# A hybrid-attention decoder layer on one core: VectorE takes the maxima of a new unit before it divides a finished one

## The reference

```
h = x @ w_in + b_in
qa, ka, va, qb, kb, vb, qc, z = split(h)
oa = banded attention(rope(qa), rope(ka), va, window 128, sinks)   # branch a, 8 heads, 2 key heads
ob = dilated attention(rope(qb), rope(kb), vb,                     # branch b, 4 heads
                       (window, stride) = (128,1), (512,4), (2048,16))
oc = attention(qc, mem @ wk, mem @ wv)                             # branch c, 4 heads, 256 keys
y  = concat(rms(oa), rms(ob), rms(oc)) * g * silu(z)
out = layer_norm(alpha * x + y @ w_out)
# within attention: s = q k / 8;  m = max(s);  p = exp(s - m);  o = (p / sum(p)) v
```

## Time and profile before

| | |
|---|---|
| median of 3 runs (lowest, highest) | 500.43 us (500.07, 501.27) |
| the profiled execution's own time | 500.67 us |
| its span, first to last instruction | 498.5 us |
| TensorE matmul busy | 488.8 us, 98% |
| VectorE busy | 311.0 us, 62% |
| ScalarE busy | 226.6 us, 45% |
| mean granted TensorE clock | 0.996 |

### The profile page before, as it was taken

How to read it: one execution, slowest core, us unless ns; L and a number is a source line. 1 busy time by engine, 2 the same in 40 slices (tenths; PEclk the granted TensorE clock), 3 DMA queues, 4 the chain that set the end, 5 groups by cost and what they waited for, 6 DMA issues and landing times.

```text
span 498.5 us, 9771 instructions
## 1 busy us (share of the span) xinstructions
PE 488.8 (98%) x3526; PEld 448.3 (90%) x3526; DVE 311.0 (62%) x893; ACT 226.6 (45%) x511; POOL 70.8 (14%) x52
## 2 busy tenths in 40 slices
PE   8999999999999999999999999999999999999994
PEld 7999999999999988888888888899888898888883
DVE  4878644557565853434534468876767868877734
ACT  5632222112211134564545659947374656454540
POOL 0000000000000000111101100023232323231414
PEclk9999999999999999999999999999999999999998
DMA  7984453547632344532331258723333424232022
GB/s 283 376 255 127 159 180 104 193 134 248 212 126 87 105 125 131 158 99 75 95 97 50 98 164 266 233 58 104 114 101 106 135 68 151 67 116 83 1 85 84
DMA packets 51838, 67.97 MB, mean 136 GB/s; under 512 B 9552, under 2 KB 41296, under 8 KB 51792
## 3 DMA queue, kind: packets, MB, share of 16 engines
q1 hardware_dynamic: 51216, 66.31, 41.6%
q10 hardware_dynamic: 576, 1.05, 0.6%
HBM read 51.31 MB, written 16.02 MB: 135 GB/s over the span
## 4 chain that ended last, share of the span: by engine, by line
PE 90%; DVE 3%; ACT 3%; DMA 1%; issue 1%; SPq 0%; DVEq 0%; ACTq 0%
PE long_ps L1032 16%; PE o_ps L979 10%; PE wide L846 8%; PE wide L845 8%; PE wide L844 8%; PE narrow L961 5%; PE long_ps L921 5%; PE long_ps L923 5%; PE long_ps L922 5%; PE wide L949 4%; PE wide L950 3%; PE wide L855 2%; PE wide L857 2%; PE wide L856 2%; DMA x_raw<-in_x_t 1%; PE narrow L1008 1%
## 5 line engine op out<-in xcount | busy, mean ns | idle before, releaser
L846 PE MATMUL wide<-x_hi,w_lo 128*128 128x256 f32 x320 | 89.6, 280 | 0.0
L844 PE MATMUL wide<-x_hi,w_hi 128*128 128x256 f32 x320 | 89.3, 279 | 0.0
L845 PE MATMUL wide<-x_lo,w_hi 128*128 128x256 f32 x320 | 89.3, 279 | 0.0
L845 PEld LDWEIGHTS wide<-x_lo,w_hi 128*128 128x128 f32 x320 | 60.2, 188 | 0.0
L846 PEld LDWEIGHTS wide<-x_hi,w_lo 128*128 128x128 f32 x320 | 60.1, 188 | 0.0
L1113 ACT ACTIVATE spill<-turn 128x512 fp32r<-128x512 f32 x21 | 13.3, 632 | 102.7 <-DVE turn L1349 76.6
L844 PEld LDWEIGHTS wide<-x_hi,w_hi 128*128 128x128 f32 x320 | 59.8, 187 | 0.0
L1622 POOL TENSOR_TENSOR g_lo<-g_raw,g_hi 128x1024 fp32r<-128x1024 f32 x6 | 14.3, 2387 | 268.5 <-ACT g_hi L1118 268.5
L1032 PE MATMUL long_ps<-wo_hi,y_hi 128*128 128x512 f32 (+1 forms) x128 | 52.2, 408 | 0.0
L1032 PE MATMUL long_ps<-wo_lo,y_hi 128*128 128x512 f32 (+1 forms) x128 | 51.4, 402 | 0.0
L1032 PE MATMUL long_ps<-wo_hi,y_lo 128*128 128x512 f32 (+1 forms) x128 | 50.8, 397 | 0.0
(11 more groups left out here) (189 smaller groups left out, 1234.4 us busy)
## 6 DMA issues: line engine op xcount, KB each, us to landing
q_spill<-spill SPq DMA_DIRECT2D x32, 256.0 KB, 2.5
q_pair<-q_spill SPq DMA_DIRECT2D x128, 64.0 KB, 2.0
w_raw<-in_w_qkv SPq DMA_DIRECT2D x12, 512.0 KB, 5.0
x_raw<-in_x_t SPq DMA_DIRECT2D x16, 256.0 KB, 8.0
g_raw<-in_w_gate SPq DMA_DIRECT2D x8, 512.0 KB, 4.1
q_pair<-q_spill SPq DMA_DIRECT2D x32, 128.0 KB, 2.8
q_pair<-q_spill SPq DMA_DIRECT2D x128, 32.0 KB, 1.8
wo_raw<-in_w_out SPq DMA_DIRECT2D x8, 512.0 KB, 4.7
```

The costliest lines, as they stand in the source:

```text
L844: pe.matmul(dst, w_hi[s][:, k, f], t_hi[:, k, cols], start=(k == 0), stop=False)
L845: pe.matmul(dst, w_hi[s][:, k, f], t_lo[:, k, cols], start=False, stop=False)
L846: mm = pe.matmul(dst, w_lo[s][:, k, f], t_hi[:, k, cols], start=False, stop=(k == KT - 1))
```

## The change

In VectorE's loop the call of `unit_max` moves ahead of the calls of `unit_out`. No instruction is added or removed, and the other engines' lists stay as they are.

```
             for v in range(ITERATIONS):
+                if 0 <= v - 1 < n_units:
+                    unit_max(v - 1)
                 for u in outs_at(v):
                     unit_out(u)
-                if 0 <= v - 1 < n_units:
-                    unit_max(v - 1)
                 if 0 <= v - 2 < n_units and two_tiles(v - 2):
                     unit_sides(v - 2)
```

## The result

The change makes the kernel slower: 518.75 us median of 4 runs (518.37 to 519.33) against 500.38 (500.07 to 501.27), ratio 1.0368, 95% interval 1.0354 to 1.0382, so 18.4 us. The forecast was 516, range 509 to 521. The profiled execution after took 519.33, 0.6 over the median, with a span of 517.2 us.

What follows compares the result with a forecast made beforehand. TensorE, with matmuls in flight 98% of the span, was taken to bound the kernel. Terms 13.2 + 2.1 + 2.0 - 1.5 = 15.8 on the profiled 500.67 gave 516.5, less 0.24, 516 us; range 509 to 521.

Steps and rivals of the forecast that it cites:

- The maxima can't begin earlier: In iteration 72, maxima start 0.83 us after the iteration's first score matmul (T), only 0.06 earlier, not the quotient's 0.65.
- Who waits: At each iteration's end times_v on TensorE waits for the quotient, as o_ps exists once; about 28 times, 15 to 20 us.
- Far units, 13.2: 16 branch-b units with merges, blocks 4 to 7: quotient behind maxima and merges delays the values' matmuls, 13.2 us together.
- ready: When the quotient reaches TensorE, counted from an iteration's first score matmul: 3.13, 3.43, 3.53, 4.13 us in blocks 4 to 7.
- Two quotients behind an a unit, 2.1: Five iterations where a pair of quotients queues behind a branch-a unit's maxima: 0.42 us each, 2.1 us.
- the rest, 2.0: Branch-a maxima with one short quotient: seven in blocks 3 to 7 at 0.15, three near 305 to 325 us at 0.35.
- Given back, 1.5 of 3.6: TensorE's eight stalls at the transposes (line 961) partly go: -1.5 us, between 0 and -3.6.
- h = 0.12: Hand-over from VectorE's quotient to TensorE's values' matmuls, taken as 0.12 us, between 0.04 and 0.3.
- Other work behind the quotient at nothing: VectorE's sides product, y product, residual sum and statistics come 0.7 later; TensorE needs them an iteration or more later: nothing.
- Rival 3: TensorE's clock falls for half of block 7 under the new stalls, which grows by 14 us: 530 us; chance 0.03.
- Blocks: Windows of the attention loop: blocks 4 to 7 longer by 2 to 3, 3 to 4, 4 to 5, 5 to 7 us.
- Rivals 1, 2, 4, 5: In order: smaller wait, 510 us, chance 0.17; larger wait, 522, 0.08; faster, 497.6, 0.02; no change, 500.4, 0.03.

Runs made afterwards that it cites:

- Far units alone: Maxima ahead of the quotient only where the new unit is a branch-b unit with merges, otherwise the kernel before: 512.44 us, ratio 1.027.
- Near units alone: Maxima ahead of the quotient everywhere except where the new unit has merges, otherwise the kernel before: 504.39 us, ratio 1.0091.
- block 7 only: Maxima ahead of the quotient only in iterations 72, 74, 76 and 78, otherwise the kernel before: 505.33 us, ratio 1.0111.
- the kernel with the stalls filled: The changed kernel plus 20 unused matmuls ahead of the values' matmuls in iterations 72, 74, 76 and 78: 518.15 us, against 518.75 for the change.
- the kernel with the maxima first where it fits: The change, with 30 of 80 iterations left in the old order, where the quotient would end too late: 501.24 us, ratio to before 1.0044.
- values after scores with the maxima first: The changed kernel with TensorE's values' matmuls moved from an iteration's end to behind the next one's scores: 496.95 us, ratio to before 0.9903.

## Why the prediction held

- *The maxima can't begin earlier.* Forecast T + 0.83, a gain of 0.06; measured T + 0.88, a gain of 0.01. Right.
- *Who waits.* Right: line 979 on TensorE, released by line 1537. Forecast about 28 times, 15 to 20 us, longest 1.5 to 1.9; shown 19 times, 12.1 us, longest 1.6 by the matmuls, and 32 times, 23.8, longest 2.0 by the weight loads. The total of neither row lies in the forecast; how much longer the iterations became is what tells.
- *Far units, 13.2.* In the changed kernel the values of the 16 far iterations start 13.4 us later in all, counted from T: 1.6, 2.7, 3.7 and 5.3 in blocks 4 to 7, against 1.5, 3.0, 3.6 and 5.1 by the sum, with its 2.2 less spread evenly. In block 7 they start at T + 4.16 or 4.17 in all four; "ready" was forecast at 4.13. So this is no luck. But these iterations became 14.6 longer: behind a wait the value matmuls take 0.88 instead of 0.80, which the sum left out. Far units alone cost 12.2 net, without the dip of 1.6, since some stalls at the transposes went.
- *Two quotients behind an a unit, 2.1, and the rest, 2.0.* The five iterations with pairs (47, 57, 67, 71, 77) grew by 2.3. Near units alone cost 3.7 net, against 4.1 less what was given back. Right within the error.
- *Given back, 1.5 of 3.6.* Waits at the transposes fell by 2.6, and the iterations that had them became 1.5 shorter in all, the dip left out. But 0.66 of that is iteration 34, which is 0.5 to 0.6 shorter also in the kernels of far units only and of block 7 only, where its order is as before. So the size agrees in part by luck; what is the change's own is nearer 1.
- *h = 0.12.* 455.87 to 456.02 is 0.15. The weight load did not pass the wait, so h did not go to zero.
- *Other work behind the quotient at nothing.* Failed in one place: the last gate tile's first matmul (line 896) waited for VectorE's gate product (line 1433) for 0.5 us, and iteration 28 took 4.83 us instead of 4.48. The cover that I named ("an iteration or more") is not there: that bank is reused at once. Cost 0.35.
- *Clock.* Rival 3 was priced as one outcome, 14 us at 3 in 100. It came true in small: iteration 73 took 4.55 us at a clock of 0.62, against 3.50 in the kernel with the stalls filled, 1.0 us. (Block 7 only took 2.95 there, but with the order of before.) A clock below 1 in blocks 4 to 7 was one of my own signs of being wrong, and on this point I was. The term should have been in the sum's range, as a small dip behind a long stall, and not only as a disaster. How much of the median's 18.4 is a dip stays open: an execution of the change with a mean clock of 0.998 took 518.37, only 0.4 below the median.
- *What the sum of 15.8 lacks to the loop's 18.0.* Far iterations 14.6 instead of 13.2, the dip 1.0 instead of nothing, pairs 2.3 instead of 2.1; the rest and what was given back come to 0.1 together instead of 0.5.
- *Blocks.* Forecast 2 to 3, 3 to 4, 4 to 5, 5 to 7 more; shown 2.2, 3.1, 5.5, 6.8. Block 6 is over. It is no backlog carried from one iteration to the next: in the same ten iterations far units alone cost 3.7 and near units alone 1.75, which add up to the 5.4 of the change (from T to T). The near units cost more than counted: iterations 63 and 70, with one quotient, 0.34 and 0.40 instead of 0.15.
- *Rivals 1, 2, 4, 5* fall: the loss of rival 1 was too small, and neither the start of the maxima nor the kernel with the maxima first where it fits shows a gain side.

## What to carry to other kernels

On an engine that takes its list in order, "first" belongs to the instruction whose input is there first, unless someone waits for the other. Before moving work off a chain of waits, look at whether it lies inside a wait of that chain: here 0.65 us of quotient lay inside the 0.83 us in which the scores were made, so it was free where it stood, and cost up to 1.8 us an iteration behind the maxima. If the order on one engine looks wrong, look at where the other engine puts the work that couples them: with the values behind the next scores, the same edit went from 18.4 us lost to 8.9 won.

## What the runs showed of the hardware

**Place of short matmuls.** With the values behind the scores the loop got faster even where nothing had ever waited: iterations 11 to 20, without a wait of TensorE over 0.2 us, are 0.75 us shorter together in both kernels. The chain of the kernel before around 232.6 us, then of the new one around 223.6 (start us, us to the next link, what):

```profile
232.49 0.11 PE o_ps L979
232.60 0.17 PE wide L949
232.77 0.12 PE wide L950
```
```profile
223.62 0.12 PE wide L949
223.74 0.12 PE wide L950
223.85 0.84 PE o_ps L979 x8
224.69 0.22 PE narrow L961 x2
```

The first 256-column score costs 0.17 behind the short value matmuls and 0.12 behind 512-column ones. In the new order the values lie between scores and transposes, and that 0.05 is gone once in each of 80 iterations, some 4 us over the loop by this row (an estimate, 80 times 0.05), though how much of the 4.1 us won in the median is this and how much the stalls at the transposes was not separated.

**The projection stage has two speeds.** From about 67 us on, the matmuls of two profiles (near units only, and values after scores with the maxima first) start every 113.3 ns on average, against 117.8 in the kernel before: 0.4 us ahead per 10.6 us, 4 us by the stage's end, at a granted clock of 1.00 in all three. The cause stays open.
